# Mixer B's sample attention: keys and values issued without waiting for constants, routing weights loaded in five pieces between its batches

## What is computed

```python
def reference(...):
    qa, ka, va, qb, kb, vb = project(x, norm1_g, w_in, ...)
    oa = diff_attn_sample(qa, ka, va, cache_k, cache_v, page_table, lam)   # mixer A
    ob = dilated_sample(qb, concat(state_b_k, kb), concat(state_b_v, vb))  # mixer B, three dilations
    h = x + concat(rms_norm(oa, subln_g) * (1 - lam_init), ob) @ w_out
    xb = rms_norm(h, norm2_g)
    q = xb @ w_q                      # PEER routing
    s = q . sub_keys                  # two times top 16, then top 16 of the pairs
    y = h + sum over picks of g * gelu(xb . u[pick]) * v[pick]
```

## Time and profile before

| | us |
|---|---|
| median of 3 runs | 3604.08 (3602.76 to 3604.13) |
| profiled execution | 3604.75 |
| its span | 3602.9 |
| PE busy / PEld busy | 3155.6 (88%) / 2641.2 (73%) |
| DVE busy | 2689.2 (75%) |
| ACT busy / POOL busy | 1182.3 (33%) / 1640.3 (46%) |
| DMA, mean over the span | 276 GB/s |

### The profile page before, as it was taken

The page is one execution under the profiler, slowest core; times in us unless marked ns, Lnnn a source line. Parts: engine busy times, 40 slices in busy tenths (PEclk is TensorE's granted clock), DMA queues, the critical chain, the costliest instruction groups (busy, mean ns, idle before and its releaser), DMA issues. The chain is left out here.

```text
span 3602.9 us, 58790 instructions
## 1 busy us (share of the span) xinstructions
PE 3155.6 (88%) x20243; PEld 2641.2 (73%) x20243; DVE 2689.2 (75%) x6413; ACT 1182.3 (33%) x2257; POOL 1640.3 (46%) x1439
## 2 busy tenths in 40 slices
PE   6999588999466988267399999999999999999998
PEld 5778345666334666267398999989989999899896
DVE  6553355333121999999489999999999999999998
ACT  5443244444112333189431322312213222122131
POOL 0000123222220588800146666666666666666665
PEclk9999799999778999699799999999999999999998
DMA  4312779888592576636899999999999999999997
GB/s 147 120 65 76 243 254 320 306 271 280 198 334 86 187 250 224 227 107 190 264 364 342 357 333 349 356 333 367 342 341 359 337 350 355 333 356 342 343 358 257
DMA packets 400256, 993.01 MB, mean 276 GB/s; under 512 B 37890, under 2 KB 160740, under 8 KB 398756
## 3 DMA queue, kind: packets, MB, share of 16 engines
q0 software_dynamic: 150048, 595.57, 46.5%
q1 hardware_dynamic: 247636, 383.53, 30.6%
q10 hardware_dynamic: 2368, 11.54, 0.8%
HBM read 911.56 MB, written 146.44 MB: 294 GB/s over the span
## 5 line engine op out<-in xcount | busy, mean ns | idle before, releaser
L2164 POOL DMA_INDIRECT uv_row<-in_v_rows,expert_tok x384 | 578.3, 1506 | 258.5 <-DVE y_tok L2346 177.8
L2203 PE MATMUL banks<-x_hi,u_hi 128*128 128x320 f32 x2048 | 633.5, 309 | 52.7 <-DVE x_lo L2292 52.5
L2164 POOL DMA_INDIRECT uv_row<-in_u_rows,expert_tok x384 | 508.5, 1324 | 302.4 <-DVE dots L2320 204.7
L2203 PE MATMUL banks<-x_lo,u_hi 128*128 128x320 f32 x2048 | 633.4, 309 | 0.0
L2203 PE MATMUL banks<-x_hi,u_lo 128*128 128x320 f32 x2048 | 633.4, 309 | 0.0
L2346 DVE SCALAR_TENSOR_TENSOR y_tok<-uv_row,share,y_tok 128x1024 f32<-128x1024 f32 x415 | 530.2, 1278 | 1.4
L2216 PE MATMUL banks<-v_hi,coef_hi 128*128 128x512 f32 x1280 | 501.6, 392 | 10.0 <-issue 8.1
L2320 DVE CUSTOM_DVE_ANT_0 uv_row<-uv_row,x_tok 128x1024 f32<-128x1024 f32 x416 | 505.7, 1218 | 0.0
L2216 PE MATMUL banks<-v_hi,coef_lo 128*128 128x512 f32 x1280 | 498.9, 390 | 0.0
L2216 PE MATMUL banks<-v_lo,coef_hi 128*128 128x512 f32 x1280 | 498.9, 390 | 0.0
L2260 ACT CAST coef_hi<-gelu 128x640 fp32r<-128x640 f32 x128 | 93.4, 730 | 1161.0 <-DVE gelu L2309 1161.0
(11 more groups left out here) (259 smaller groups left out, 5544.7 us busy)
## 6 DMA issues: line engine op xcount, KB each, us to landing
keys_ps<-in_cache_k SPq DMA_DIRECT2D x256, 256.0 KB, 4.7
values_ps<-in_cache_v POOLq DMA_DIRECT2D x256, 256.0 KB, 4.6
uv_raw<-in_u SPq DMA_DIRECT2D x128, 512.0 KB, 7.6
uv_raw<-in_v SPq DMA_DIRECT2D x128, 512.0 KB, 7.8
scratch_gates<-stage SPq DMA_DIRECT2D x10, 4096.0 KB, 23.6
gates<-scratch_gates SPq DMA_DIRECT2D x128, 320.0 KB, 6.4
out_win_k_out<-in_state_k POOLq DMA_DIRECT2D x8, 4088.0 KB, 21.7
out_win_v_out<-in_state_v POOLq DMA_DIRECT2D x8, 4088.0 KB, 14.9
```

The costliest lines, as they stand in the source:

```text
L2164: pool.indirect_dma_start(out=rows[n % ROWS][:, :], out_offset=None, in_=io["u_rows" if kind == "u" else "v_rows"], in_offset=bass.Indirec ...
L2203: ins = nc.tensor.matmul(bank[:, 2 * r + c, 0:CH], u[r][a][:, k * P:(k + 1) * P], x2[b][:, k, c * CH:(c + 1) * CH], start=(k == 0 and a == b),
```

## The change

For mixer "b", SP and POOL no longer wait for the six constants before the first key and value load; PE and DVE still do. ACT no longer issues the three weight loads at its start. Its turns are written out, and behind the exponentials of batches 1 and 3 it issues one half of `w_out` each, behind those of batches 5 and 6 one half of `w_q` each, and behind those of batch 7 `sub_keys`. Its last wait counts five loads (80) instead of three (48).

```diff
             sp.dma_start(sel[:, :, :], io[f"sel_{mixer}"]).then_inc(consts_loaded, 16)
-            sp.wait_ge(consts_loaded, 96)
+            if a:
+                sp.wait_ge(consts_loaded, 96)
...
-            pool.wait_ge(consts_loaded, 96)
+            if a:
+                pool.wait_ge(consts_loaded, 96)
             for c in range(C):
                 load_v(0, c)
...
-            if weights:
-                load_route_weights(act, io, weights, weights_loaded)
+            w_out, w_q, sub_keys = weights
             exps(0)
-            def turn_of(b):
+            for b in range(DB - 1):
                 take_exps_T(b)
                 exps(b + 1)
-
-            turns(act, DB - 1, turn_of)
+                if b in (0, 2):
+                    half = slice(KD // 2 * (b // 2), KD // 2 * (b // 2 + 1))
+                    act.dma_start(w_out[:, half, :], io["w_out"].rearrange("(k p) c -> p k c", p=P)[:, half, :]).then_inc(weights_loaded, 16)
+                if b in (4, 5):
+                    half = slice(KD // 2 * (b - 4), KD // 2 * (b - 3))
+                    act.dma_start(w_q[:, half, :], io["w_q"].rearrange("(k p) c -> p k c", p=P)[:, half, :]).then_inc(weights_loaded, 16)
+            act.dma_start(sub_keys[:, :, :, :], io["sub_keys"]).then_inc(weights_loaded, 16)
             take_exps_T(DB - 1)
-            if weights:
-                act.wait_ge(weights_loaded, 48)
+            act.wait_ge(weights_loaded, 80)
```

More of the change, by code:

```diff
@@ L1318, in move_state @@
     pool.dma_start(out[b, STATE - DQ:, :], new[SEQ + b * DQ:SEQ + (b + 1) * DQ, :]).then_inc(moved, 16)
[L1321 to L1326, removed]
 def mix_and_route(nc, io, sems, ident, bank, weights, chosen, picksT, tiles):
```

## The result

The changed kernel takes 3613.13 us (median of 9 runs, 3610.4 to 3617.04) against 3604.13 us (9 runs, 3601.69 to 3606.77): ratio 1.0024, 95% interval 1.0015 to 1.0033. It is 9 us slower; 10 us faster was forecast. The profiled execution has a span of 3611.3 us, 8.4 more than the 3602.9 of before.

A forecast was written before the change was run, and what follows sets the result against it. The prediction held the stage short of DMA time, not of an engine. An earlier start (23.7 us) less longer turns (11.8) less the tail (1.5) gave a gain of 10.4 us: 3593.7 against 3604.08, range 3588.0 to 3601.0.

The forecast's parts named there:

- The stage: Mixer B's sample attention, 129.90 us long behind which all engines meet a barrier; its gain or loss moves the end equally.
- The first exponentials: Start of the stage: batch 0's exponentials begin at 985.8 instead of 1009.50, gain 23.7 us, bounds 18.8 and 25.0.
- The tail: After the last exponentials: batch 7's values alternate with sub-keys and the rest of w_q, loss 1.5 us, bounds 0 and 4.
- The issues of ACT: Between batches: each weight piece costs ACT an issue of 0.45 to 0.65 us, hidden in its idle time.
- The rate of 0.405 MB/us: Stage's loads: the rate at which the DMA engines deliver, used to turn bytes into time at the start and in turns.
- the costing of the turns: Seven turns between batches' exponentials: each the larger of its length or byte time, 82.65 against 70.82, loss 11.8 us.
- Its own sign: Turns with weights: the forecast is wrong if PE's waits for values add up to more than 5 us each.
- The first one: Turns between batches: the values' round trip stretches them; full form 3610.7, chance 0.03, mild form 3603.8, chance 0.10.
- its full form: Weighted turns: values land last, 14 us of bytes plus about 4 until the last request, 18 us; 3610.7, chance 0.03.
- Late constants: Start of the stage: constants need their full 6.9 us alone with keys behind them, gain 5.5, 3598.6; chance 0.09.
- A lower rate of the engines: Turns and start: loads run at 0.370 MB/us, not 0.405, costing 7.1 us together, 3600.8; chance 0.10.
- The weights fit into gaps: Turns: the PE, DVE, ACT chain may set their length and DMA take more; gain 17.6, 3586.5; chance 0.12.

## Why the prediction was wrong

**What held.** The stage, and that its gain or loss passes one to one to the end: the rest stayed within 1.5 us. The prediction allowed 1 and called more a sign of being wrong, but the rest of nearly one program wanders by 3.6 us over the kernels here, so this sign was set too tight. The first exponentials: 985.8 forecast, 986.16 measured. The tail: 1.5 forecast, 1.74 measured. The issues of ACT (0.35 to 0.39 us each) hold nobody. The rate of 0.405 MB/us as what the engines can give, though not as what the change drew from them: its long turns ran at 296 to 372 GB/s.

**The step that failed** is the costing of the turns, "each turn by the larger of its own length and its bytes". It gave 82.65 us; 99.36 were measured. Its own sign came true: PE's waits for values in turn 2 add up to 8.0 us, where more than 5 was to mean that it is wrong. By pairs, since the lateness falls into the turn behind the piece: turns 1 and 2, 23.5 forecast and 30.65 measured; 3 and 4, 24.1 and 30.44; 5 and 6, 26.45 and 28.69; turn 0, 8.6 and 9.58. The larger of two is right only where loads and work overlap, and that needs requests that go out before the work they are for has begun. One batch of buffers allowed this in the kernel before with a margin of about a microsecond (in turn 5, v_new was issued at 1065.15 and used at 1070.46, with 4.4 us to land in the median), and the piece of weights used that up. Behind it the two terms add. That the turns took 82.3 us with two batches of buffers, close to the 82.65 of the forecast, is chance: two of those turns were 16 us long by the wait for the output store, and without it all seven took 73.5.

**The rivals.** The first one named the mechanism and came nearest: 3610.7 for its full form, 3613.13 measured, with a chance of 0.03. Its full form took the turn as 14 us of bytes and 4 to the last request, 18; measured are 20 to 21.5, since behind the late values comes the whole chain to the next exponentials, 12 us, not 4. That its sum for the turns (27.7 us) comes so near to the measured 28.5 is in part luck: it lengthened four turns, and three long ones were measured. What I put against it ("three of the four value pieces are requested before the weight piece") is not so: the first is issued at 995.53, the weights at 995.75, the second and third from 996.24 on. The kernel before had shown the same order, with values issued at 1017.92 and from 1018.63 on around exponentials at 1018.12. It would have meant little anyway, since the queues take turns by packets, as the text had shown itself at its start. The price was written down and the chance not drawn from it: a median landing of 4.4 us with a wait for v_new already present left no slack for a third stream.

Late constants did not occur. A lower rate of the engines did not either: what the long turns lack is requests, and with buffers the same engines gave 405. "The weights fit into gaps" was the opposite of what happened to this kernel, which could not even use what it had. Its reading that a share of 0.99 can still take more was right: with two outputs the share read 1.03, at 405 GB/s instead of 370.

**The chances.** Faster by over 0.2% had 0.72, slower 0.04; it came out slower by 0.24%, outside the range of 3588 to 3601.

## What to carry to other kernels

A transfer added to a loop costs its bytes only if the loop's own requests are out early enough; with one set of buffers each request waits for the use of the one before, and then a competing stream costs its lateness and the whole chain behind it, with the DMA engines idle meanwhile. So before filling "free" DMA time, compare the landing time of the last load of a turn with the moment of its use; where the slack is a microsecond, add buffers first. Here they were worth 17 us with the weights left where they were, and after them the place of the weights within the phase no longer showed in the time, while moving bytes out of the phase did.

## What the runs showed of the hardware

Queues in use together moved about equal numbers of packets (195 and 183; 148, 150 and 131), so what a stream takes from another goes by its packets, not by who asked first; moving the halves from ACT's queue to SP's, with sub_keys a turn earlier, was worth 7 us. Loads at 405 to 409 GB/s with a share of 1.03 were seen in four turns running, 8.5 to 14.2 us long. The section "Where 436 GB/s comes from" of the Trainium skill's page "DMA: Bandwidth & Descriptors" puts loads from HBM at about 358 GB/s for a core; these four turns were 13 to 14% above it.

The constants, some 1400 packets, were in 16.8 us after the phase's first load beside the weights (969.82 to 986.64), 10.1 us beside the values (969.88 to 979.98 in the changed kernel), and 5.1 us alone (968.56 to 973.66 in the kernel with the wait kept). So beside the weights some 12 of the 16.8 us were their turn behind large packets. The forecast had put 2 us for the stretch in which the last 900 run alone and 0.7 as the least; alone, the 1490 packets of that queue took no more than the 5.1.

In turn 2 of the changed kernel the granted clock fell from 2.4 to 1.2 GHz (PEclk 1.00 to 0.50) while PE waited for values, working 0.12 us in the two from 1007, and it came back after PE had been busy for all of the two from 1023; the work between took 11.8 us, where it takes 8.6 at 2.4 GHz in turn 5.
